# Gate and up products of two feed-forward networks with the weights as the stationary operand

## The chip, the cores and the metric

The kernel runs on one core of one Trainium2 chip. The metric is the device time of one execution in microseconds. Three runs of the kernel before gave a median of 2644.72 us (2642.13 to 2646.27). Traces come from one profiled execution, whose span, from the first to the last instruction, is 2638.1 us.

## What is computed

Two transformer blocks run one after the other on 256 tokens of width 2048, in float32. Each ends with a gated feed-forward network of hidden width 5632, and only these two networks are touched by the change:

```python
h2 = _rms(x, g_norm2) * (1 + sc2) + sh2                      # first block
gate, up = jnp.split(h2 @ w_ffn_in, 2, axis=-1)
x = x + gt2 * ((jax.nn.silu(gate) * up) @ w_ffn_out)
...
v = rmsnorm(h, ffn_norm_w)                                   # second block
h = h + (jax.nn.silu(v @ w_gate) * (v @ w_up)) @ w_down
return rmsnorm(h, final_norm_w)
```

## The kernel before

Names: P = 128, SEQ = 256 tokens, T = 2 token tiles of 128, CW = 512 columns, KD = 16 blocks of the width 2048, KF = 44 blocks of the hidden width.

**Split products.** Every float32 product is made of three fp32r products: operands are split into a high part, rounded to fp32r, and a low rest, and hi*hi, lo*hi and hi*lo are added in PSUM. A `Gemm` goes through chunks of 512 weight columns, and a chunk through slots of two 128-row blocks of the weights (k = 0, 1). A slot's raw weights (512 KB) are loaded by SyncE's queue into one of four buffers, ScalarE makes `w_hi` (`weights_high`, four buffers), VectorE makes `w_lo` (`weights_low`, two buffers). TensorE then issues 12 matmuls of a slot (lines 501 to 511): per k and token tile two with `w_hi` (token parts hi and lo), then per k and token tile one with `w_lo`. The tokens (`g.lhs`, 128 x 128) are the stationary operand and 512 weight columns stream past them. Output is 128 tokens by 512 columns, one PSUM bank for each token tile; chunks take turns between banks 0, 1 and banks 2, 3. With one chunk in flight, TensorE begins chunk c + 2 only when the banks of chunk c were read (line 487).

**Order.** Every engine runs its own hand-written instruction list; semaphores order them. What reads a finished chunk hangs as a hook in the list of ScalarE or VectorE, ahead of the weight conversion of slot `hook_at` = 4 of the following chunk. Chunks are written out one by one (`peeled` pairs) and then in a loop over pairs of chunks (`Fori`, line 103).

**The networks** (`Ffn`, line 1465). `self.g` has 22 chunks of 8 slots each, gate and up in turn: even chunks are gate, odd ones up. In the first network 5 pairs are written out and 6 go through the loop, in the second 2 and 9. The hook of a gate chunk (ScalarE, line 1572) writes silu(bank) to `ftmp`; that of an up chunk (VectorE, lines 1591 to 1597) writes `hbuf` = bank * `ftmp`, tokens on partitions. The product `self.down` (4 chunks of 22 slots) needs the hidden values with the hidden width on partitions, so `fill` (line 1551) makes TensorE turn the 8 blocks of a pair into `ps_turn`, in slot 2 of the next up chunk (`middle`, line 492), the last pair's in slot 4 of `down`. ScalarE's `high` and VectorE's `low` split what was turned into `ht_hi` and `ht_lo`. In the second network the tokens' inverse root mean square is left out of the product and is multiplied in when gate and up chunks are read, as a scalar per partition. ScalarE computes its squares beside slot 7 of the first chunk.

Of the kernel before, what the change touches and what calls it, by code (L numbers as in the profile page):

```python
# [11 lines left out]
ALU = mybir.AluOpType  # L12
# [33 lines left out]
class Gemm:  # L46


    def __init__(self, at, weights, k, n, lhs, cols=None, peeled=PEELED, k0=0):
# [11 lines left out]
        self.hook_at = min(4, 3 * self.S // 4)  # L61
# [83 lines left out]
def program(nc, A, out):  # L145
# [258 lines left out]
    def scalar_gemm(act, g, evac, carried=None, ahead=0):  # L404
# [7 lines left out]
        def chunk(u, j, before):  # L412
            for s, w in g.slots(u, j):
                if s == g.hook_at and before and g.S != 2:
# [41 lines left out]
    def tensor_gemm(pe, g, middle=None):  # L456
# [26 lines left out]
        def chunk(u, j, before):  # L483
# [4 lines left out]
            for s, w in g.slots(u, j):  # L488
# [3 lines left out]
                if s == g.S // 4 and before and middle:  # L492
                    middle(u - 1, j)
# [6 lines left out]
                pe.wait_ge(hi_ready, (w + 1).value)  # L500
                for k in range(2):
                    for t in range(T):
                        for part in range(2):
                            pe.matmul(bank[t][:, :], g.lhs(part, g.k0 + 2 * s + k, t), w_hi[:, w % HI, k, :],  # L504
                                      start=(s == 0 and k == 0 and part == 0), stop=False)
                pe.wait_ge(raw_used, (w + 1).value)
                for k in range(2):
                    for t in range(T):
                        mm = pe.matmul(bank[t][:, :], g.lhs(0, g.k0 + 2 * s + k, t), w_lo[:, w % LO, k, :],  # L509
                                       start=False, stop=(s == g.S - 1 and k == 1))  # L510
                mm.then_inc(w_used, 1)
# [3 lines left out]
        return lambda: middle(g.n - 1, None)  # L515
# [155 lines left out]
    def row_tensor(pe, n, bank):  # L671
        pe.wait_ge(diag_ready, 2 * n + 2)
        pe.matmul(bank[:, 0:SEQ], ones, diag[:, :, :].rearrange("p t q -> p (t q)"),
                  start=True, stop=True).then_inc(row_filled, 1)

    def diag_vector(dve, inv):
        for t in range(T):
            dve.tensor_scalar(diag[:, t, :], ident, inv(t), None, ALU.mult).then_inc(diag_ready, 1)

    def row_vector(dve, n, bank):  # L680
        dve.wait_ge(row_filled, n + 1)
        dve.tensor_copy(inv_row[:, :], bank[:, 0:SEQ]).then_inc(row_ready, 1)
# [721 lines left out]

    def evac_out(c, u, j):
# [19 lines left out]
    KF = 5632 // P  # L1425
    ht_hi = place("ht_hi", GT1, [KF, SEQ], F32R)
# [38 lines left out]
    class Ffn:  # L1465
# [4 lines left out]
        def __init__(self, name, w_gate, w_up, up0, w_down, scale, bias, gate, source=None, peeled=2):  # L1470
# [5 lines left out]
            self.g = Gemm(at, None, KD, 2 * KF // 4, lhs_x, cols=at_pair, peeled=peeled)  # L1476
            self.g.by_half = (w_gate, w_up)
            self.g.needs = self.turn.ready
            if source:
# [3 lines left out]
                turned_act, turned_dve = self.g.beside.act, self.g.beside.dve  # L1483
# [11 lines left out]
                self.g.beside.act, self.g.beside.dve = act_beside, dve_beside  # L1495
# [3 lines left out]
            self.at, self.at_split = turns["n"], turns["split"]  # L1499
            turns["n"] += KF // 2  # L1500
            turns["split"] += KF // 2
            self.down = Gemm(at, w_down, KF, 4, lhs_h, peeled=2)
            evac_down = evac_residual(self.down, gate)
# [8 lines left out]
            def down_needs(pe, s):  # L1512
                pe.wait_ge(turn_scaled, self.at + min(s + 1, KF // 2))

            def down_pe(pe, u, s):
                if (u, s) == (0, 4):
                    self.fill(pe, last_pair, Count(self.g.c + self.g.n))

            def down_act(act, u, s):
                if (u, s) == (0, 2) and gate is not None:  # L1520
                    gate_load(act, 1, gate)
                if (u, s) == (0, 7):
                    self.high(act, last_pair)

            def down_dve(dve, u, s):
                if (u, s) == (0, 7):
                    self.low(dve, last_pair)
            self.down.needs = down_needs
            self.down.beside.pe, self.down.beside.act, self.down.beside.dve = down_pe, down_act, down_dve

        def unit(self, pair, v):
            return (Count(self.at + 2 * pair.first + v, 2 * pair.per, pair.j),
                    Count(self.at_split + 2 * pair.first + v, 2 * pair.per, pair.j),
                    Count(4 * pair.first + 2 * v, 4 * pair.per, pair.j).value)

        def high(self, act, pair):
            for v in range(2):
                n, m, k = self.unit(pair, v)
                act.wait_ge(turn_filled, (n + 1).value)
                act.activation(ht_hi[:, bass.ds(k, 2), :].rearrange("p a b -> p (a b)"), ps_turn[v][:, :],  # L1540
                               ACT.Copy).then_inc(turn_hi, 1)

        def low(self, dve, pair):
            for v in range(2):
                n, m, k = self.unit(pair, v)
                dve.wait_ge(turn_hi, (m + 1).value)
                dve.tensor_tensor(ht_lo[:, bass.ds(k, 2), :].rearrange("p a b -> p (a b)"), ps_turn[v][:, :],
                                  ht_hi[:, bass.ds(k, 2), :].rearrange("p a b -> p (a b)").bitcast(F32),
                                  ALU.subtract).then_inc(turn_scaled, 1)

        def fill(self, pe, pair, c_end):
            pe.wait_ge(evac_done, c_end.value)
            for v in range(2):
                n, m, _ = self.unit(pair, v)
                pe.wait_ge(turn_scaled, (n - v).value)
                for k in range(2):
                    for t in range(T):
# [1389 lines left out]
```

## Time and profile before

| | |
|---|---|
| median of 3 runs | 2644.72 us |
| profiled execution, span | 2638.1 us |
| TensorE matmul busy | 98% of the span |
| TensorE weight load busy | 80% |
| VectorE busy | 63% |
| ScalarE busy | 45% |
| DMA | 212 GB/s mean over the span |
| granted TensorE clock, mean | 0.998 of 2.4 GHz |

Busy time of TensorE is modelled, since matmuls are pipelined: the distance from one start to the next is what tells its pace. "PEld" is TensorE's loading of a stationary operand, which runs beside the matmul before it. The chain of waits is the sequence of work that ended last, from the last instruction back to the first.

### The profile page before, as it was taken

How to read it: one execution, taken by the hardware profiler on the slowest of the kernel's cores; microseconds unless marked ns; L12 is line 12 of the kernel's file. 1: busy time of each engine (PE TensorE's matmuls, PEld its weight loads, DVE VectorE, ACT ScalarE, POOL GpSimd, SP SyncE). 2: the span in 40 equal slices, each digit the busy share in tenths (PEclk: the TensorE clock that was granted, in tenths of full speed). 3: DMA queues.
4: the chain of work that ended last, by engine and by line, in shares of the span. 5: the costliest groups of instructions: out<-in, count | busy, mean ns of one | idle time of the engine just before them, and what ended most of it. 6: DMA issues, size and time to landing. Idle time of an engine off the chain costs nothing.

```text
span 2638.1 us, 33116 instructions
## 1 busy us (share of the span) xinstructions
PE 2582.3 (98%) x12027; PEld 2118.6 (80%) x12027; DVE 1669.4 (63%) x2308; ACT 1194.3 (45%) x1595; POOL 149.2 (6%) x211
## 2 busy tenths in 40 slices
PE   5999999999999999999999999999999999999998
PEld 3888887878788888888888888776888888888887
DVE  7888998889877745454445664657645454454444
ACT  3543337644444444444334554446454444444443
POOL 1221111111111000000000000000000000000000
PEclk9999999999999999999999999999999999999999
DMA  9998994868788766666555655530666666665554
GB/s 347 318 304 268 312 320 155 283 203 314 250 265 279 244 185 191 189 189 203 194 194 185 188 171 178 172 116 17 183 184 191 191 186 191 189 190 188 195 192 168
DMA packets 269020, 559.41 MB, mean 212 GB/s; under 512 B 22800, under 2 KB 24544, under 8 KB 268256
## 3 DMA queue, kind: packets, MB, share of 16 engines
q1 hardware_dynamic: 235216, 454.23, 54.7%
q0 software_dynamic: 26752, 96.48, 11.0%
q10 hardware_dynamic: 6928, 7.07, 0.8%
q8 instruction: 75, 1.23, 0.2%
q14 instruction: 49, 0.40, 0.0%
HBM read 555.60 MB, written 2.11 MB: 211 GB/s over the span
## 4 chain that ended last, share of the span: by engine, by line
PE 94%; DVE 2%; ACT 1%; DMA 1%; issue 1%; SPq 0%; ACTq 0%; DVEq 0%
PE ps L504 57%; PE ps L509 28%; PE ps L545 1%; PE ps L1558 1%; DMA first_raw<-in_w_ada 1%; PE ps L2555 1%; PE ps L359 1%; PE ps L2402 1%; DMA ada_raw<-in_w_ada 1%; PE ps L2585 0%; PE ps L281 0%; SPq L319 0%; PE ps L2565 0%; PE ps L1269 0%; PE ps L2584 0%
## 5 line engine op out<-in xcount | busy, mean ns | idle before, releaser
L401 DVE TENSOR_TENSOR w_lo<-raw,w_hi 128x1024 fp32r<-128x1024 f32 x846 | 1033.7, 1223 | 824.5 <-PE ps L509 752.0
L395 ACT ACTIVATE w_hi<-raw 128x1024 fp32r<-128x1024 f32 x846 | 895.0, 1062 | 1146.8 <-PE ps L509 476.4
L504 PE MATMUL ps<-w_hi,xt_hi 128*128 128x512 f32 x2488 | 981.4, 394 | 4.8 <-ACT w_hi L395 1.6
L504 PE MATMUL ps<-w_hi,xt_lo 128*128 128x512 f32 x2488 | 969.8, 390 | 0.0
L509 PE MATMUL ps<-w_lo,xt_hi 128*128 128x512 f32 x2488 | 666.6, 390 | 3.9 <-DVE w_lo L401 3.9
L504 PEld LDWEIGHTS ps<-w_hi,xt_hi 128*128 128x128 f32 x2488 | 467.3, 188 | 105.6 <-issue 6.4
L509 PEld LDWEIGHTS ps<-w_lo,xt_hi 128*128 128x128 f32 x2488 | 466.5, 188 | 104.0 <-DVE w_lo L401 6.0
L504 PEld LDWEIGHTS ps<-w_hi,xt_lo 128*128 128x128 f32 x2488 | 467.6, 188 | 93.6
L504 PE MATMUL ps<-w_hi,ht_hi 128*128 128x512 f32 x696 | 271.6, 390 | 0.0
L504 PE MATMUL ps<-w_hi,ht_lo 128*128 128x512 f32 x696 | 270.9, 389 | 0.0
L509 PE MATMUL ps<-w_lo,ht_hi 128*128 128x512 f32 x696 | 186.1, 389 | 0.0
L319 POOL DMA_DIRECT2D ada_raw<-in_w_ada x192 | 138.8, 723 | 752.6 <-DVE acc_odd L343 588.7
L509 PEld LDWEIGHTS ps<-w_lo,ht_hi 128*128 128x128 f32 x696 | 130.7, 188 | 27.2
L504 PEld LDWEIGHTS ps<-w_hi,ht_hi 128*128 128x128 f32 x696 | 130.7, 188 | 26.9
L504 PEld LDWEIGHTS ps<-w_hi,ht_lo 128*128 128x128 f32 x696 | 130.7, 188 | 26.9
L343 DVE SCALAR_TENSOR_TENSOR acc<-ada_raw,ccol,acc 128x512 f32<-128x512 f32 (+1 forms) x171 | 119.9, 701 | 2.6 <-DMA ada_raw<-in_w_ada 2.5
L343 DVE SCALAR_TENSOR_TENSOR acc_odd<-ada_raw,ccol,acc_odd 128x512 f32<-128x512 f32 (+1 forms) x171 | 119.8, 701 | 0.0
L504 PE MATMUL ps<-w_hi,yt_hi 128*128 128x512 f32 x128 | 51.7, 404 | 0.0
L504 PE MATMUL ps<-w_hi,yt_lo 128*128 128x512 f32 x128 | 50.0, 391 | 0.0
L2799 POOL DMA_DIRECT2D w1k<-in_cmp_w_k x4 | 3.0, 752 | 732.9 <-PE ps L509 732.9
L1064 DVE TENSOR_TENSOR proj<-ps,proj 128x512 f32<-128x512 f32 x64 | 41.0, 681 | 3.1 <-PE ps L509 3.1
L2644 ACT ACTIVATE pb<-pb,nst 128x128 f32<-128x128 f32 x64 | 28.5, 447 | 29.6 <-DVE nst L2620 29.6
(398 smaller groups left out, 1590.1 us busy)
## 6 DMA issues: line engine op xcount, KB each, us to landing
raw<-in_w_in SPq DMA_DIRECT2D x208, 512.0 KB, 4.7
raw<-in_w_ffn_in SPq DMA_DIRECT2D x176, 512.0 KB, 4.1
ada_raw<-in_w_ada POOLq DMA_DIRECT2D x128, 512.0 KB, 5.6
raw<-in_w_ffn_out SPq DMA_DIRECT2D x88, 512.0 KB, 4.3
raw<-in_w_gate SPq DMA_DIRECT2D x88, 512.0 KB, 3.7
raw<-in_w_up SPq DMA_DIRECT2D x88, 512.0 KB, 4.4
raw<-in_w_down SPq DMA_DIRECT2D x88, 512.0 KB, 3.6
raw<-in_w_out SPq DMA_DIRECT2D x64, 512.0 KB, 4.7
```

Of the source, the lines that this page charges most:

```text
L319: sp.dma_start(self.tile(v), wview("w_ada")[:, ADA_K * s:ADA_K * (s + 1), col:col + width]).then_inc(ada_first[v] if v < 2 * self.per else ...
L343: ins = dve.scalar_tensor_tensor(part, rows[:, k, :], weight, part, ALU.mult, ALU.add)
L359: mm = pe.matmul(ps_ada[:, at_i:at_i + 1], acc[:, b % 2, i * P:(i + 1) * P], ones[:, 0:1], start=True, stop=True)
L395: act.activation(w_hi[:, w % HI, :, :], raw[:, w % RAW, :, :], ACT.Copy).then_inc(hi_ready, 1)
L401: dve.tensor_tensor(w_lo[:, w % LO, :, :], raw[:, w % RAW, :, :], w_hi[:, w % HI, :, :].bitcast(F32), ALU.subtract).then_inc(raw_used, 1)
L504: pe.matmul(bank[t][:, :], g.lhs(part, g.k0 + 2 * s + k, t), w_hi[:, w % HI, k, :], start=(s == 0 and k == 0 and part == 0), stop=False)
L509: mm = pe.matmul(bank[t][:, :], g.lhs(0, g.k0 + 2 * s + k, t), w_lo[:, w % LO, k, :], start=False, stop=(s == g.S - 1 and k == 1))
L545: mm = pe.transpose(ps_turn[n % 3][:, k * SEQ + t * P:k * SEQ + (t + 1) * P], self.src(2 * v + k, t), ident)
L1064: last = nc.vector.tensor_tensor(p, ps_gemm[2 * (c % 2) + t][:, :], p, ALU.add)
L1558: mm = pe.transpose(ps_turn[v][:, k * SEQ + t * P:k * SEQ + (t + 1) * P], hbuf[:, t, (2 * v + k) * P:(2 * v + k + 1) * P], ident)
L2402: mm = pe.matmul(ps_ada[0:60, 0:256], fl[i][:, u, :, :].rearrange("p h i -> p (h i)"), w1[i][:, u, :], start=(u == 0), stop=(u == 15))
L2644: act.activation(pb2[:, i % 4, lo:up], pb2[:, i % 4, lo:up], ACT.Exp, bias=nst[:, 1, 2 * i + t:2 * i + t + 1], scale=nsa_scale, accum_out= ...
```

## The change

In the gate and up products of both networks the operands change places. A 128 x 128 block of the weights is loaded as the stationary operand, and the 256 tokens of one 128-row block of the turned input stream past it. A slot is now 24 matmuls with 256 streamed columns each, in `turned`, in place of 12 with 512. A PSUM bank then holds two 128-column blocks of output, each 128 hidden columns by 256 tokens, so the output comes out turned. `fill`, `middle` and the turns are gone; `high` and `low` read `hbuf` in SBUF and are in other hooks: `high` of a pair in the next gate chunk's hook (first network) or in its own up chunk's (second network), `low` in the next gate chunk's. The last pair's are beside slots 4 and 5 of `down`, or in its carried hook.

In the second network tokens are now along the free axis, so their inverse root mean square is made into a row: two diagonal blocks on VectorE and one fp32 matmul by ones on TensorE in slot 0 of the second chunk, one copy on VectorE. VectorE multiplies gate chunks by that row into `ftmp`, ScalarE does silu in place, VectorE multiplies by the up chunk; the up side's factor is put off to the reading of `down` (`evac_scaled`, `final_add`). VectorE's hook is at slot 2 and ScalarE's at slot 6 there.

```diff
+        def turned(bank, s, w):
+            out = lambda m: bank[m // 2][:, m % 2 * SEQ:(m % 2 + 1) * SEQ]
+            pe.wait_ge(hi_ready, (w + 1).value)
+            for k in range(2):
+                for m in range(4):
+                    for part in range(2):
+                        pe.matmul(out(m), w_hi[:, w % HI, k, m * P:(m + 1) * P], g.turned(part, g.k0 + 2 * s + k),
+                                  start=(s == 0 and k == 0 and part == 0 and m % 2 == 0), stop=False)
+            pe.wait_ge(raw_used, (w + 1).value)
+            for k in range(2):
+                for m in range(4):
+                    mm = pe.matmul(out(m), w_lo[:, w % LO, k, m * P:(m + 1) * P], g.turned(0, g.k0 + 2 * s + k),
+                                   start=False, stop=(s == g.S - 1 and k == 1 and m % 2 == 1))
+            mm.then_inc(w_used, 1)
...
-                if s == g.S // 4 and before and middle:
-                    middle(u - 1, j)
...
+                (turned if g.turned else straight)(bank, s, w)
...
+    def evac_scaled(g, inv):
+
+        def evac(c, u, j):
+            for t in range(T):
+                xc = x[:, t, bass.ds(Count(CW * u, 2 * CW, j).value, CW)]
+                last = nc.vector.scalar_tensor_tensor(xc, ps_gemm[2 * (c % 2) + t][:, :], inv(t), xc, ALU.mult, ALU.add)
+            last.then_inc(evac_done, 1)
+        return evac
...
-            self.g = Gemm(at, None, KD, 2 * KF // 4, lhs_x, cols=at_pair, peeled=peeled)
+            self.g = Gemm(at, None, KD, 2 * KF // 4, None, cols=at_pair, peeled=peeled)
+            self.g.turned = lambda part, k: (xt_lo if part else xt_hi)[:, k, :]
...
+                self.g.hook_at, self.g.act_hook_at = 2, 6
...
+                def pe_beside(pe, u, s):
+                    turned_pe(pe, u, s)
+                    if (u, s) == (1, 0):
+                        row_tensor(pe, 2, ps_ada, diag2)
...
-                    if (u, s) == (1, 2):
-                        self.rms.vector(dve)
+                    if (u, s) == (1, 0):
+                        diag_vector(dve, self.rms.vector(dve), diag2)
...
             def down_needs(pe, s):
-                pe.wait_ge(turn_scaled, self.at + min(s + 1, KF // 2))
+                pe.wait_ge(self.h_lo, min(s + 1, KF // 2))
...
-        def fill(self, pe, pair, c_end):
-            pe.wait_ge(evac_done, c_end.value)
-            for v in range(2):
-                n, m, _ = self.unit(pair, v)
-                pe.wait_ge(turn_scaled, (n - v).value)
-                for k in range(2):
-                    for t in range(T):
-                        mm = pe.transpose(ps_turn[v][:, k * SEQ + t * P:k * SEQ + (t + 1) * P],
-                                          hbuf[:, t, (2 * v + k) * P:(2 * v + k + 1) * P], ident)
-                mm.then_inc(turn_filled, 1)
...
             def evac(c, u, j):
+                if u % 2:
+                    return
+                act.wait_ge(evac_done, c.value)
+                for v in range(2):
+                    last = act.activation(ftmp[:, v, :], ps_gemm[2 * (c % 2) + v][:, :], ACT.Silu)
+                last.then_inc(evac_done, 1)
+                if j is not None or u > 0:
+                    self.high(act, Count(u // 2 - 1, 1, j))
+
+            def evac_scaled_gate(c, u, j):
+                act.wait_ge(evac_done, (c + 1).value)
                 if u % 2 == 0:
...
+                    for v in range(2):
+                        last = act.activation(ftmp[:, v, :], ftmp[:, v, :], ACT.Silu)
+                    last.then_inc(self.silu_done, 1)
+                else:
+                    self.high(act, Count(u // 2, 1, j))
...
+                pair = Count(u // 2, 1, j)
                 if u % 2 == 0:
+                    if j is not None or u > 0:
+                        self.low(dve, pair - 1)
+                    if self.source:
+                        if j is None and u == 0:
+                            row_vector(dve, 2, ps_ada, inv_row2)
+                        else:
+                            dve.wait_ge(evac_done, c.value)
+                        for v in range(2):
+                            last = dve.tensor_tensor(
+                                ftmp[:, v, :].rearrange("p (m q) -> p m q", m=2),
+                                ps_gemm[2 * (c % 2) + v][:, :].rearrange("p (m q) -> p m q", m=2),
+                                inv_row2[:, None, :].broadcast_to([P, 2, SEQ]), ALU.mult)
+                        last.then_inc(evac_done, 1)
                     return
...
-            def middle(u, j):
-                if u % 2 == 0 and (j is not None or u > 0):
-                    self.fill(pe, Count(u // 2 - 1, 1, j), Count(self.g.c + u, 2, j))
-            tensor_gemm(pe, self.g, middle)()
+            tensor_gemm(pe, self.g)
             tensor_gemm(pe, self.down)
```

## Rows read from the trace of the kernel before

**Rows 1.** The page: busy times (1), the chain that ended last (4).

```profile
PE 2582.3 (98%) x12027; PEld 2118.6 (80%) x12027; DVE 1669.4 (63%) x2308; ACT 1194.3 (45%) x1595; POOL 149.2 (6%) x211
...
PE 94%; DVE 2%; ACT 1%; DMA 1%; issue 1%; SPq 0%; ACTq 0%; DVEq 0%
```

**Rows 2.** Chain of waits, first network's loop: start us, us, what.

```profile
1014.39 1.83 PE ps L504 x8
...
1018.94 0.91 PE ps L509 x4
1019.84 1.81 PE ps L504 x8
1021.66 0.91 PE ps L509 x4
...
1057.93 0.87 PE ps L1558 x8
1058.81 1.38 PE ps L504 x6
```

**Rows 3.** Line 1558 alone: durations ns min/median/max, first and last start.

```profile
L1558 PE MATMUL ps<-const,hbuf x176: 270/273/274, 788.2 to 2403.7; 128*128 128x128 f32 x176
```

**Rows 4.** Chain of waits around the narrow products of line 281.

```profile
405.22 2.73 PE ps L281 x24
407.95 0.87 PE ps L545 x8
408.82 2.76 PE ps L281 x24
```

**Rows 5.** Chain of waits, the second narrow product.

```profile
1544.10 5.46 PE ps L281 x48
```

**Rows 6.** Timeline, TensorE's matmuls and then its loads: start us, us, instruction.

```profile
1549.28 0.28 PE L281 MATMUL ps<-xt_lo,w_in_rest_hi 128*64 128x256 f32 x1
1549.39 0.40 PE L504 MATMUL ps<-w_hi,xt_hi 128*128 128x512 f32 x1
...
1549.28 0.19 PEld L504 LDWEIGHTS ps<-w_hi,xt_hi 128*128 128x128 f32 x1
```

**Rows 7.** Timeline, 930.2 to 931.2: a small load beneath a 512-column matmul.

```profile
930.01 0.84 PE L509 MATMUL ps<-w_lo,xt_hi 128*128 128x512 f32 x3
930.69 0.27 PE L959 MATMUL ps<-const,acol 128*16 128x128 f32 x1
```

**Rows 8.** Timeline, 830 to 831: loads of 128 columns, one streamed column each.

```profile
829.92 0.86 PEld L359 LDWEIGHTS ps<-const,acc 128*128 128x128 f32 x7
```

**Rows 9.** Timeline of ScalarE, VectorE and TensorE, start of the second network.

```profile
1921.77 0.30 ACT L716 ACTIVATE stat<-stat,epsc 128x2 f32<-128x2 f32 x1
...
1923.05 2.36 DVE L401 TENSOR_TENSOR w_lo<-raw,w_hi 128x1024 fp32r<-128x1024 f32 x2 [4.11 <-PE ps L509]
1926.27 1.23 DVE L401 TENSOR_TENSOR w_lo<-raw,w_hi 128x1024 fp32r<-128x1024 f32 x1 [0.86 <-PE ps L509]
1927.41 0.16 DVE L726 RECIPROCAL stat<-stat 128x2 f32<-128x2 f32 x1
...
1926.00 0.39 PE L504 MATMUL ps<-w_hi,xt_hi 128*128 128x512 f32 x1
```

**Rows 10.** Lines 673, 678 and 682, the same steps for another norm.

```profile
L673 PE MATMUL ps<-diag,const x4: 379/431/483, 33.2 to 710.3; 128*128 128x256 f32 x4
...
L678 DVE TENSOR_SCALAR diag<-const,stat x4: 280/284/288, 32.6 to 709.6; 128x128 f32<-128x128 f32 x4
...
L682 DVE COPY inv_row<-ps x2: 416/420/423, 35.1 to 710.7; 128x256 f32<-128x256 f32 x2
```

**Rows 11.** Groups by line, second network's loop: busy us, mean ns, idle before.

```profile
L395 ACT ACTIVATE w_hi<-raw 128x1024 fp32r<-128x1024 f32 x154 | 163.7, 1063 | 244.1 <-PE ps L509 154.4 <-DMA raw<-in_w_up 85.6 <-DMA raw<-in_w_gate 4.0
L1572 ACT ACTIVATE ftmp<-ps,stat 128x512 f32<-128x512 f32 x18 | 11.2, 675 | 0.0
L1540 ACT ACTIVATE ht_hi<-ps 128x512 f32 (+1 forms) x20 | 10.7, 584 | 0.0
...
L401 DVE TENSOR_TENSOR w_lo<-raw,w_hi 128x1024 fp32r<-128x1024 f32 x154 | 188.5, 1224 | 215.2 <-PE ps L509 213.7 <-ACT w_hi L395 1.5
L1594 DVE SCALAR_TENSOR_TENSOR hbuf<-ps,stat,ftmp 128x512 f32<-128x512 f32 x20 | 14.0, 743 | 0.0
L1547 DVE TENSOR_TENSOR ht_lo<-ps,ht_hi 128x512 f32 (+1 forms) x20 | 12.8, 679 | 0.0
```

**Rows 12.** DMA view: TensorE's instruction queue (packets, MB), two DMA issues (KB, us to landing).

```profile
q8 instruction: 75, 1.23, 0.2%
...
w2k<-in_cmp_w_k ACTq DMA_DIRECT2D x1, 64.0 KB, 7.4
const<-in_const SPq DMA_DIRECT2D x1, 128.0 KB, 2.2
```

**Rows 13.** Line 103, the loops' ends, on TensorE's sequencer.

```profile
L103 PEldq COMPARE_BRANCH  x15: 76/208/231, 982.4 to 2385.6; - x15
```

More of the change, by code:

```diff
@@ L413, in chunk @@
             for s, w in g.slots(u, j):
-                if s == g.hook_at and before and g.S != 2:
+                if s == g.act_hook_at and before and g.S != 2:
                     hook(u - 1, j)
@@ L454, in vector_gemm, with tensor_gemm, straight @@
         return lambda: hook(g.n - 1, None)
-    def tensor_gemm(pe, g, middle=None):
+    def tensor_gemm(pe, g):
+        def turned(bank, s, w):
[12 more added lines that the diff above has]
+            mm.then_inc(w_used, 1)
+        def straight(bank, s, w):
+            pe.wait_ge(hi_ready, (w + 1).value)
+            for k in range(2):
+                for t in range(T):
+                    for part in range(2):
+                        pe.matmul(bank[t][:, :], g.lhs(part, g.k0 + 2 * s + k, t), w_hi[:, w % HI, k, :],
+                                  start=(s == 0 and k == 0 and part == 0), stop=False)
+            pe.wait_ge(raw_used, (w + 1).value)
+            for k in range(2):
+                for t in range(T):
+                    mm = pe.matmul(bank[t][:, :], g.lhs(0, g.k0 + 2 * s + k, t), w_lo[:, w % LO, k, :],
+                                   start=False, stop=(s == g.S - 1 and k == 1))
+            mm.then_inc(w_used, 1)
         def by_tokens(c, u, w):
@@ L499, in chunk @@
                     g.needs(pe, s)
-                pe.wait_ge(hi_ready, (w + 1).value)
-                for k in range(2):
-                    for t in range(T):
[L503 to L511, printed above, removed]
+                (turned if g.turned else straight)(bank, s, w)
                 if j is None:
@@ L1403, in program @@
     evac_out1 = evac_residual(g_out, gt1)
+    def evac_scaled(g, inv):
+        def evac(c, u, j):
+            for t in range(T):
+                xc = x[:, t, bass.ds(Count(CW * u, 2 * CW, j).value, CW)]
+                last = nc.vector.scalar_tensor_tensor(xc, ps_gemm[2 * (c % 2) + t][:, :], inv(t), xc, ALU.mult, ALU.add)
+            last.then_inc(evac_done, 1)
+        return evac
     def evac_out(c, u, j):
@@ L1425, in program @@
     KF = 5632 // P
+    diag2 = place("diag2", SCR + 5120, [T, P])
+    inv_row2 = place("inv_row2", SCR + 4096, [SEQ])
     ht_hi = place("ht_hi", GT1, [KF, SEQ], F32R)
@@ L1521, in down_act @@
                     gate_load(act, 1, gate)
-                if (u, s) == (0, 7):
+                if (u, s) == (0, 4) and not source:
+                    act.wait_ge(evac_done, self.g.c + self.g.n)
                     self.high(act, last_pair)
             def down_dve(dve, u, s):
-                if (u, s) == (0, 7):
+                if (u, s) == (0, 5):
                     self.low(dve, last_pair)
             self.down.needs = down_needs
-            self.down.beside.pe, self.down.beside.act, self.down.beside.dve = down_pe, down_act, down_dve
+            self.down.beside.act, self.down.beside.dve = down_act, down_dve
         def unit(self, pair, v):
-            return (Count(self.at + 2 * pair.first + v, 2 * pair.per, pair.j),
-                    Count(self.at_split + 2 * pair.first + v, 2 * pair.per, pair.j),
+            return (Count(2 * pair.first + v + 1, 2 * pair.per, pair.j),
                     Count(4 * pair.first + 2 * v, 4 * pair.per, pair.j).value)
@@ L1584, in evac @@
             def evac(c, u, j):
+                pair = Count(u // 2, 1, j)
                 if u % 2 == 0:
[L1586 to L1597 removed]
+                    if j is not None or u > 0:
[11 more added lines that the diff above has]
+                        last.then_inc(evac_done, 1)
+                    return
+                if self.source:
+                    dve.wait_ge(self.silu_done, (pair + 1).value)
+                else:
+                    dve.wait_ge(evac_done, c.value)
+                for v in range(2):
+                    last = dve.tensor_tensor(hbuf[:, v, :], ps_gemm[2 * (c % 2) + v][:, :], ftmp[:, v, :], ALU.mult)
                 last.then_inc(evac_done, 1)
[L1599 to L1600 removed]
             last = vector_gemm(dve, self.g, evac, carried, 0)
```

74 lines of the change are left out of this document (22 added, 52 removed).

## Prediction

> **What bounds the kernel now.** I read the page's busy times first, then its chain of waits: TensorE's matmuls are busy 98% of the span and 94% of the chain is TensorE [rows 1]. So only what TensorE does, or what makes it wait, counts; VectorE at 63% and ScalarE at 45% are cover as long as they stay ahead. Then I read the chain in order of time inside the first network's loop, for the pace. A slot of gate or up takes 1.81 + 0.91 = 2.72 us for 12 matmuls with 512 streamed columns, 226.7 ns each [rows 2]. A pair of chunks, from one group of turns to the next, takes 1058.81 - 1014.39 = 44.42 us, and 16 slots are 43.52 us, so 8 turns with the transitions around them cost 0.90 us [rows 2]. The change has three questions: what goes with the turns, what the new shape of matmul costs, and whether anything new is late.
>
> **Turns removed.** 176 turns are 22 groups of 8 [rows 3]. They stand in TensorE's own list with nothing beside them: 22 x 0.90 = 19.8 us off the path.
>
> **24 matmuls of 256 columns for 12 of 512.** There are 2 x 22 x 8 = 352 slots and the streamed columns stay at 6144, but the loads of a stationary 128 x 128 block double. No row has 256 fp32r columns over a 128-column load in a run, so I bound the pace from both sides.
> - Stream: line 281 streams 256 fp32r columns over 64-column loads, 5.46 us for 48, or 113.75 ns each, as in the first 24 of another [rows 4, 5]; 24 right behind turns took 2.76 us, 115.0 ns each [rows 4]. Half of 226.7 is 113.3, so the cost is nearly all per column. Over all 96 the mean is 10.95 / 96 = 114.06 ns.
> - Load: with one streamed column above them, seven loads of 128 columns take 0.86 us, a last one 0.19 us, so they follow each other at (0.86 - 0.19) / 6 = 112 ns [rows 6, 8]. This is just below the stream's 113.3.
> - Do they nest? At the end of line 281 a 128-column load of line 504 starts with a 256-column matmul at 1549.28, and the next matmul starts at 1549.39, 0.11 us later [rows 6]. In the opposite case the third of three 512-column matmuls has a load of only 16 columns beneath it, and the three still take 0.68 us, 227 ns each [rows 7]. So a lighter load doesn't quicken the stream and a heavier one, once, didn't slow it.
>
> The pace is the larger of 113.3 and 112, with a little for jitter in so tight a fit. I take 113.5 ns, between a half of 226.7 and the 113.75 that holds a few slower starts: 24 x 113.5 - 2720 = 4 ns a slot, 352 slots, +1.3 us. Ends: 113.3 gives 0, and 116.5 gives (2796 - 2720) x 352 = +26.8 us.
> The Trainium skill, "TensorE: Matmul & The Clock Gate", section "Back-to-back issue gap", speaks against the change: a warm matmul takes its columns at 2.4 GHz and a fixed 2.5 ns. By that a slot would gain 12 x 2.5 = 30 ns, an estimate of +10.6 us. The trace shows 227 and 114 ns, where the page would have 216 and 109; as 512a + f and 256a + f they give f = 2 x 114.06 - 226.7 = 1.4 ns.
>
> **The row in the second network.** TensorE gets one fp32 matmul by ones; the same form took 379 to 483 ns [rows 10]: +0.45 us. It also gets a wait for VectorE's diagonals, and all its later matmuls are queued behind that. The root is done at 1922.07 and slot 0 of the second chunk ends at 1926.00 [rows 9]. VectorE makes the first `w_lo` from 1923.05 to 1924.27, then 0.16 for the reciprocal and 2 x 0.28 for the diagonals: 1925.0, 1.0 us ahead of need [rows 9, 10]. The next `w_lo` slips by 0.7 us and is still done at 1926.2, while its matmuls start 1.81 us into the slot. The copy of the row takes 0.42 us on VectorE and waits for TensorE's matmul at about 1926.9; it and two multiplications end near 1928.8, and the `w_lo` behind them at 1930.0, needed at 1931.0. All hidden, bounds 0 to +1 us.
>
> **VectorE's and ScalarE's hooks.** They cost 0, and the cover is this. VectorE can start a `w_lo` when the slot two before it ends, 2.72 + 1.81 us ahead of need; less its 1.22 us that leaves 3.3 us. The heaviest new hook (second network, gate) is two `low` at 0.68 and two multiplications by a row, a form not in the trace, between 0.68 and 0.74 each: 2.84 us [rows 11]. It starts 1.22 us into the chunk and ends at 4.06, where the next `w_lo` could have begun at 2.72: 1.34 of the 3.3 us are used. In the first network a hook has two instructions on VectorE, before it had four. ScalarE is up to four slots ahead, and its heaviest hook, four activations of about 0.58 us, takes 2.3 of more than 9 us; silu from SBUF is not shown, but silu and copies from PSUM took 0.58 to 0.68 [rows 11]. A gate result now passes VectorE, ScalarE, VectorE, with 8 slots for it. SyncE's loads wait for `w_lo` as before; ScalarE's idle time before `w_hi` ends partly on DMA [rows 11], with slots in hand. Reading `down` costs 0.74 in place of 0.68 us, hidden save for the last one at the end: +0.05 us. If this cover were gone, each hook's overrun would count 22 times.
>
> **Sum.** -19.8 + 1.3 + 0.45 + 0.05 = -18.0 us against the profiled span of 2638.1, or 2620.1. Around the span lie 2644.72 - 2638.1 = 6.6 us to the median of the runs, which stay: 2627 us.
>
> **Rivals.**
> - *Each matmul has a fixed part after all.* f from 1.4 to 6 ns, times 4224 additional matmuls, is +5.9 to +25 us in place of 1.3: 2632 to 2651. For it: 115.0 ns behind turns is f = 3.3 [rows 4], and only 1 ns lies between load and stream. Against it: 48 in a row at 113.75 [rows 5]. From f = 4.6 ns nothing is left of the gain. At the page's 2.5 ns it is 2636. Chance 0.20.
> - *The load slows the stream: slower than before.* 226.7 is 13.4 ns above 512 columns at 2.4 GHz, and 113.75 about 7 above 256. The matmul of 512 has a load of 128 columns and that of 256 one of 64, so the surplus could come from the load. Then 256 over 128 is 106.7 + 13.4 = 120 ns, +160 ns a slot, +56 us: 2682. It decides from 115.6 ns on. Against it stand the two single cases of [rows 6, 7]. Chance 0.08.
> - *The loop no longer stays in instruction memory: slower too.* A loop turn grows from 16 x 24 + 16 = 400 loads and matmuls to 768. Of 24,054 executed [rows 1], 13 repeats of 400 leave 18,850, and the queue brought 1.23 MB [rows 12], which is 65 bytes for each of these: repeats were not fetched again, and the branch takes 208 ns [rows 13]. How much more is held no row shows. A miss at each of 13 branches costs one transfer, 2.2 to 7.4 us [rows 12]: +29 to +96 us, 2656 to 2723. The skill's page "Runtime: NRT & Kernel Launch", section "Instruction fetch mechanics", has a taken branch stall when its target is out of a two-page window, with pages of 256 instructions, but gives TensorE room for 2048. By the window the old loop of 400 was near the limit and the new one is beyond it; by the room it fits. Chance 0.07.
> - *A new wait*, on the diagonals or behind the 2.84 us hook: once up to 3 us, or 22 times up to 1 us, 2628 to 2649. Chance 0.05.
> - *The turns go but other transitions of TensorE stay*, some 3 us less gain: 0.02.
>
> **Numbers.** The forecast, 2625 to 2632 (pace 113.3 to 114.06), has 0.58. Under 2622 there is almost nothing, since 19.8 us is all that is removed. The range goes up to 2654, over the fixed part and the new wait; the two slow cases, 0.15, stay out. About 0.2%, 5.3 us, is what a measurement can tell from no change. Faster: 0.58 + 0.08 of the fixed part + 0.03 of the new wait + 0.02 = 0.71. Same: 0.09 + 0.02 = 0.11. Slower: 0.03 + 0.08 + 0.07 = 0.18.
>
> **What would show it.** No turn of `hbuf`; 8448 matmuls of 128x256 in gate and up with starts 113 to 114 ns apart, a slot still 2.72 us and a pair 43.5; no idle time of TensorE ended by VectorE at the start of the second network; TensorE's instruction queue silent inside the loops. A slot of 2.77 us would be the fixed part, 2.88 the load, a gap of some us once a loop turn the instructions.

## The result, and the profile after

The kernel after takes 2681.26 us (median of 4 runs, 2678.53 to 2681.91), that before, beside it, 2645.32 us: a ratio of 1.0136, with a 95% interval of 1.0121 to 1.015. The change costs 36 us, where 18 us of gain were forecast. The profiled execution has a span of 2679.2 us. It is 41.1 us over that of before, but 5 of these lie ahead of the changed code: the row matmul of the norm before the first network starts at 715.2 us, that of before at 710.3 [rows 10]. The program up to there is the same; from 25 to 75 us TensorE's granted clock was 0.86 of full speed in this execution, part of it at 1.2 GHz, and 1.00 in that of before.

The page of after, busy times, the chain that ended last and TensorE's instruction queue, as [rows 1, 12]:

```profile
PE 2625.6 (98%) x16077; PEld 2328.4 (87%) x16077; DVE 1685.5 (63%) x2333; ACT 1192.8 (45%) x1595; POOL 149.5 (6%) x211
...
q8 instruction: 88, 1.44, 0.2%
...
PE 96%; DVE 1%; ACT 1%; DMA 1%; issue 1%; SPq 0%; ACTq 0%; DVEq 0%
```

The chain of waits in the first network's loop, as [rows 2] (line 465 is the products with `w_hi`, line 470 those with `w_lo`):

```profile
1016.11 1.92 PE ps L465 x16
1018.03 0.96 PE ps L470 x8
1018.99 1.92 PE ps L465 x16
1020.91 0.96 PE ps L470 x8
```

There are no turns between chunks any more, and no gap. But a slot takes 1.92 + 0.96 = 2.88 us for 24 matmuls, 120.0 ns each, in place of 2.72. It does so from the first chunk of the first network to the last of the second: 352 x 0.16 = 56.3 us more, less 19.8 us for the turns, is 36.5 us, the whole loss. The costliest groups of loads and matmuls (busy us, mean ns of one, idle time before):

```profile
L465 PE MATMUL ps<-xt_hi,w_hi 128*128 128x256 f32 x2816 | 692.3, 284 | 1.0 <-issue 1.0
...
L465 PEld LDWEIGHTS ps<-xt_hi,w_hi 128*128 128x128 f32 x2816 | 540.4, 192 | 1.5 <-issue 1.4
...
L479 PEld LDWEIGHTS ps<-w_hi,xt_hi 128*128 128x128 f32 x1080 | 204.1, 189 | 51.3 <-ACT w_hi L396 5.6
```

In the products that kept their form (line 479) TensorE's loading side has idle time before its instructions; in the turned ones (line 465) it has next to none, 1.5 us over 2816 loads. That alone doesn't tell what sets the pace: the run load_64 below, at 113.3 ns a matmul, has next to none either. No matmul of gate and up waits for VectorE or ScalarE. The new steps at the start of the second network, VectorE's timeline, answer to [rows 9]: the copy of the row waits 0.90 us for TensorE, the two multiplications take 0.64 each, and the `w_lo` behind them makes nobody wait.

```profile
1950.50 0.42 DVE L698 COPY inv_row<-ps 128x256 f32<-128x256 f32 x1 [0.90 <-PE ps L689]
1950.96 1.29 DVE L1618 TENSOR_TENSOR ftmp<-ps,inv_row 128x512 f32<-128x512 f32 x2
1952.16 2.43 DVE L402 TENSOR_TENSOR w_lo<-raw,w_hi 128x1024 fp32r<-128x1024 f32 x2
```

### The profile page after: what moved, and what is told of

It reads as the page before. It is cut to its first block, busy times and chain, and to the rows that moved or that the text cites. A ratio compares the mean times of both kernels' runs of the same rounds, so it can differ in the third digit from the quotient of the medians.

```text
span 2679.2 us, 41186 instructions
## 1 busy us (share of the span) xinstructions
PE 2625.6 (98%) x16077; PEld 2328.4 (87%) x16077; DVE 1685.5 (63%) x2333; ACT 1192.8 (45%) x1595; POOL 149.5 (6%) x211
## 3 DMA queue, kind: packets, MB, share of 16 engines
q8 instruction: 88, 1.44, 0.2%
## 4 chain that ended last, share of the span: by engine, by line
PE 96%; DVE 1%; ACT 1%; DMA 1%; issue 1%; SPq 0%; ACTq 0%; DVEq 0%
PE ps L479 33%; PE ps L465 25%; PE ps L484 16%; PE ps L470 13%; PE ps L561 1%; DMA first_raw<-in_w_ada 1%; PE ps L2581 1%; PE ps L360 1%; PE ps L2428 1%; PE ps L2611 0%; SPq L320 0%; PE ps L282 0%; PE ps L2591 0%; PE ps L2610 0%; PE ps L2026 0%
## 5 line engine op out<-in xcount | busy, mean ns | idle before, releaser
L465 PE MATMUL ps<-xt_hi,w_hi 128*128 128x256 f32 x2816 | 692.3, 284 | 1.0 <-issue 1.0
L465 PE MATMUL ps<-xt_lo,w_hi 128*128 128x256 f32 x2816 | 690.8, 283 | 0.0
L465 PEld LDWEIGHTS ps<-xt_hi,w_hi 128*128 128x128 f32 x2816 | 540.4, 192 | 1.5 <-issue 1.4
L465 PEld LDWEIGHTS ps<-xt_lo,w_hi 128*128 128x128 f32 x2816 | 540.5, 192 | 0.1
L479 PE MATMUL ps<-w_hi,xt_hi 128*128 128x512 f32 x1080 | 431.7, 400 | 5.8 <-ACT w_hi L396 4.7
L479 PE MATMUL ps<-w_hi,xt_lo 128*128 128x512 f32 x1080 | 423.2, 392 | 0.0
L470 PE MATMUL ps<-xt_hi,w_lo 128*128 128x256 f32 x2816 | 395.3, 283 | 0.0
L470 PEld LDWEIGHTS ps<-xt_hi,w_lo 128*128 128x128 f32 x2816 | 363.3, 192 | 0.0
L484 PE MATMUL ps<-w_lo,xt_hi 128*128 128x512 f32 x1080 | 289.8, 390 | 0.8 <-DVE w_lo L402 0.8
L484 PEld LDWEIGHTS ps<-w_lo,xt_hi 128*128 128x128 f32 x1080 | 203.0, 188 | 44.5 <-DVE w_lo L402 1.4
```

Source lines behind the costliest of these rows:

```text
L465: pe.matmul(out(m), w_hi[:, w % HI, k, m * P:(m + 1) * P], g.turned(part, g.k0 + 2 * s + k), start=(s == 0 and k == 0 and part == 0 and m ...
L470: mm = pe.matmul(out(m), w_lo[:, w % LO, k, m * P:(m + 1) * P], g.turned(0, g.k0 + 2 * s + k), start=False, stop=(s == g.S - 1 and k == 1 ...
```

## The experiments

The theory was now the rival of 0.08: the surplus over pure streaming (13.3 ns for each matmul) is paid by every matmul above a 128-column load, however few columns it streams. Against it stood other causes for the same 2.88 us: twice the instructions, the turned form's addresses or banks, the removal of the turns itself.

**pace: TensorE alone.** Series of matmuls of one shape each, with nothing beside them.

```diff
+            for i in range(2 * N):        # N = 240; series of other sizes alike
+                pe.matmul(ps[i % 4][:, 0:256], wr[:, at(i, 128):at(i, 128) + 128], xr[:, 0:256], start=True, stop=True)
+            for i in range(2 * N):
+                pe.matmul(ps[i % 4][0:64, 0:256], wr[:, at(i, 128):at(i, 128) + 64], xr[:, 0:256], start=True, stop=True)
```

> Nothing of the kernel is computed here: TensorE alone runs series of 240 or 480 independent matmuls, each with its own stationary load, and the distance of starts in each is read. Theory A, the surplus belongs to the loaded columns: a matmul of N streamed fp32r columns with S stationary ones takes N / 2.4 + S / 9.6 ns. Theory B, a load of 128 columns needs 120 ns and the stream 1.0625 x N / 2.4, and the larger counts. Theory C, TensorE's instruction stream gives one instruction in 60 ns, so a load and a matmul take at least 120 ns. N=512: S=128 all 226.7; S=64 A 220, B and C 226.7; S=32 A 216.7, B and C 226.7. N=384, S=128: A 173.3, B and C 170. N=256: S=128 all 120; S=96 A 116.7, B 113.3, C 120; S=64 A and B 113.3, C 120; S=32 A 110, B 113.3, C 120. N=128, S=128: A 66.7 or the load's 112, B 120, C 120. bf16 with 128 stationary columns, 512 and 256 streamed: 215.5 and 109 by rows of the kernel before where only the first is shown; C 120 for the second. Alternating 128 and 64 stationary columns at N=256 tells which matmul of the two carries the surplus.

It took 658.54 us. Its chain of waits, one piece a series (start us, us, matmuls):

```profile
39.88 31.28 PE ps L50 x138
```

```profile
71.61 55.20 PE ps L52 x240
126.81 55.60 PE ps L54 x240
182.41 41.62 PE ps L56 x240
224.03 57.59 PE ps L58 x480
281.62 27.84 PE ps L60 x240
309.46 54.41 PE ps L62 x480
363.87 27.20 PE ps L64 x240
391.07 28.79 PE ps L66 x240
419.86 26.22 PE ps L68 x240
```

```profile
623.08 26.75 PE ps L87 x240
```

Each line divided by its count gives the distance of two starts. fp32r, 512 streamed columns: 226.7 ns over a load of 128 (line 50), 230.0 over 64 (line 52), 231.7 over 32 (line 54). 384 over 128: 173.4 (line 56). 256 columns: 120.0 over 128 (line 58), 116.0 over 96 (line 60), 113.35 over 64 (line 62), 113.3 over 32 (line 64); with the same block loaded each time 120.0 (line 66). bf16, 256 over 128: 109.25 (line 68). fp32r, 128 over 128: 111.5 (line 87). So 120.0 and 113.35 ns both come back with TensorE alone: the loss has nothing to do with this kernel's queues, banks or DMA. The row of line 281 that the forecast went by is right, for its loads of 64 columns.

None of the three theories holds throughout. C is out, since 116.0 and 113.35 ns lie under its 120. B is out by 384 columns (173.4 against 170) and by 96 loaded ones (116.0 against 113.3). A is within 1 ns for loads of 64 to 128 columns beneath 256, and for 384 over 128. But at 32 loaded columns it gives 110 where 113.3 was measured, and at 512 streamed ones it has narrower loads quicken the stream, 220 and 216.7, where they slow it, 230.0 and 231.7. The alternating series (lines 73 and 75, 256 columns) should have told whether a surplus goes with a matmul's own width or with the load beneath it. By the start times the next matmul comes 116.4 ns behind a 128-wide one with a 64-column load beneath it, and 117.0 ns behind a 64-wide one with a 128-column load beneath it. Both are near the mean of 120.0 and 113.35, so the series doesn't tell. In every series the load and the matmul that uses it are equally wide, so "width of the load" below always means both.

**no_turns: the change without its form.** The turns stay out, but gate and up products keep the old form, tokens loaded and 512 weight columns streamed.

```diff
-            self.g = Gemm(at, None, KD, 2 * KF // 4, None, cols=at_pair, peeled=peeled)
-            self.g.turned = lambda part, k: (xt_lo if part else xt_hi)[:, k, :]
+            self.g = Gemm(at, None, KD, 2 * KF // 4, lhs_x, cols=at_pair, peeled=peeled)
```

> The changed kernel with the old form of matmul in gate and up (tokens stationary, 512 streamed columns); its output is not the reference's, since what is read as turned is not turned. It has the turns removed, the row and the new hooks. If the step on the turns was right, it takes 2645.3 - 19.8 + 0.5 = 2626 us, and the whole loss of the change, 2681.3 - 2626 = 55 us, is the form of the matmuls. If hooks or the new wait cost something, it is above 2626 by that much.

2624.67 us (2622.4 to 2626.39), ratio 0.9929 (0.9908 to 0.9949). Its chain in the loop:

```profile
1001.20 1.81 PE ps L479 x8
1003.01 0.91 PE ps L484 x4
1003.92 1.81 PE ps L479 x8
```

The slot is 2.72 us again and the gain of the turns is there: 17 us under the 2641.84 of before beside it, 13 to 24 by the interval. The new hooks, the row and the wait are in this kernel too, and cost nothing that shows: 2626 was expected with 0.5 us for them. The loss, 57 us from here to after, is the matmul's form.

**load_96: 96 of 128 weight columns.** The turned products load 96 columns and so make 96 of 128 hidden columns; all else stays.

```diff
-                        pe.matmul(out(m), w_hi[:, w % HI, k, m * P:(m + 1) * P], g.turned(part, g.k0 + 2 * s + k),
+                        pe.matmul(out(m)[0:96], w_hi[:, w % HI, k, m * P:m * P + 96], g.turned(part, g.k0 + 2 * s + k),
```

> The changed kernel with only 96 of each 128 weight columns loaded in gate and up, so a quarter of the hidden values is not computed; number of matmuls, streamed columns, waits and DMA stay. Theory A (surplus per loaded column): 116.7 ns, 24 x 3.33 x 352 = 28 us less than 2681: 2653. Theory B (load-bound): 113.3 ns, 56 us less: 2625. Theory C (instruction stream): 120 ns, 2681.

2647.93 us (2641.41 to 2655.8), ratio 1.0021 (1.0008 to 1.0033).

```profile
1001.43 1.85 PE ps L465 x16
1003.28 0.93 PE ps L470 x8
```

2.78 to 2.79 us a slot, 116 ns a matmul, the 116.0 of line 60. Same instructions, addresses and streamed columns as after, with fewer loaded columns: the time falls by 33 us. It is nearest to theory A, by which the surplus grows with the loaded columns (2653), 5 us below it.

**half_the_loads: hi and lo tokens over one load.** They lie next to each other, and one load of a `w_hi` block is followed by one matmul with 512 streamed columns: 8 matmuls of 512 and 8 of 256 in a slot. The first block (k = 0) of each chunk's first slot keeps its pairs of 256, 4 of the 8 pairs of one slot in eight.

```diff
-                    for part in range(2):
-                        pe.matmul(out(m), w_hi[:, w % HI, k, m * P:(m + 1) * P], g.turned(part, g.k0 + 2 * s + k),
-                                  start=(s == 0 and k == 0 and part == 0 and m % 2 == 0), stop=False)
+                    if s == 0 and k == 0:
+                        for part in range(2):
+                            pe.matmul(out(m), w_hi[:, w % HI, k, m * P:(m + 1) * P], g.turned(part, g.k0 + 2 * s + k),
+                                      start=(part == 0 and m % 2 == 0), stop=False)
+                        continue
+                    pe.matmul(bank[m // 2][:, :], w_hi[:, w % HI, k, m * P:(m + 1) * P],
+                              xt_both[:, :, g.k0 + 2 * s + k, :], start=False, stop=False)
```

> The changed kernel with the high and the low part of the tokens streamed as one matmul of 512 columns over one load of w_hi, into a whole bank; the two halves are not added, so the output is not the reference's. A slot has 8 matmuls of 512 and 8 of 256 columns: 16 loads in place of 24. Theory A: 8 x 226.7 + 8 x 120 = 2773 ns in place of 2880, 38 us less than 2681: 2644. Theory B: a load beneath 512 columns is free, one beneath 256 takes 120, also 2773 ns and 2644. Theory C: 8 x 226.7 + 8 x 120 as well, or 2720 ns and 2625 if the queue evens the pairs out. It tells what the change would cost with its loads shared.

2650.11 us (2647.77 to 2652.32), ratio 1.0024 (1.0014 to 1.0034).

```profile
1000.25 1.84 PE ps L469 x8
1002.09 0.95 PE ps L474 x8
1003.04 1.84 PE ps L469 x8
```

Nearly a third fewer matmuls over 128 columns take 31 us off, where 37 were expected. The pairs that stay are 44 x 4 x 13.3 ns = 2 us of the difference. The price per matmul holds for most of the rest. The matmuls of 512 took 230 ns here and not 226.7, which is 8 x 3.3 ns x 352 = 9 us; those of 256, at 119 and not 120, give 3 of them back. In the kernel before the eight matmuls of 512 behind the turns are slower in the same way, 1.83 us where later slots have 1.81 [rows 2], and the first five behind line 281's [rows 6] start 229 to 236 ns apart. So a change of shape or type seems to slow the matmuls of 512 behind it, and here one comes in every slot. No run varies that alone.

**pace2: what the surplus belongs to.** TensorE alone again: other lengths, plain fp32, 64 partitions, accumulation in one bank with moving addresses, and bf16 and fp32r by turns, in which load and matmul above it are of different types.

```diff
+            for i in range(N):
+                if i % 2:
+                    pe.matmul(ps[i % 4][:, 0:256], wr[:, at(i, 128):at(i, 128) + 128], xr[:, 0:256], start=True, stop=True)
+                else:
+                    pe.matmul(ps[i % 4][:, 0:256], wb[:, at(i, 128):at(i, 128) + 128], xb[:, 0:256], start=True, stop=True)
```

> Nothing of the kernel is computed; series of 240 matmuls of TensorE alone, as in the run pace. That run showed a surplus over N / 2.4 of 13.3 ns for fp32r with 128 loaded columns at N = 256, 384 and 512, a distance of 112 ns at N = 128, and only 2.5 ns for bf16. Theory D, shared reading: an fp32r stream takes TensorE's whole reading rate, so what a load of 128 fp32r columns reads beneath it comes on top, 13.3 ns, and a stream that leaves room (bf16, fp32 in its passes) hides it. Theory A, own load: the surplus belongs to the fp32r matmul itself, whatever is loaded beneath. Taking turns of bf16 and fp32r, N=256: D 112 for the bf16 matmul (the fp32r load beneath it limits) and 107 to 110 for the fp32r matmul (light bf16 load beneath it), about 220 for two; A 109 + 120 = 229 or, limited by the load, 232. The same at N=512: D 215.5 + 215 to 220, A 215.5 + 226.7 = 442. fp32r, 128 loaded columns: N=192 the load's 112 (80 + 13.3 = 93 is hidden), N=224 112 (93.3 + 13.3 = 106.7), N=320 146.7 by both. fp32 N=256: 215 to 219 a pass, as line 2555 in the kernel before. 112 loaded columns at N=256: 118.3 if in proportion. 64 partitions in place of 128: 120 by both. One bank with accumulation and moving source addresses: 120 by both, other than 120 if the surplus is a matter of addresses or banks. One bf16 in three at N=256: D 112 + 120 + 109, A 109 + 2 x 120 = 349.

```profile
101.64 26.78 PE ps L60 x240
128.42 26.82 PE ps L62 x240
155.24 35.20 PE ps L64 x240
190.44 51.80 PE ps L66 x240
242.24 28.27 PE ps L68 x240
270.50 28.98 PE ps L70 x240
299.49 28.98 PE ps L72 x240
```

192 columns over 128 take 111.6 ns (line 60), 224 take 111.75 (line 62), 320 take 146.7 (line 64). 256 over 112 loaded take 117.8 (line 68). The plain fp32 series issues 120 matmuls of 256 columns and its trace has 240, so each runs as two of 215.8 ns, 431.7 together (line 66). Neither 64 partitions (line 70) nor one bank and moving addresses (line 72) change the 120 ns: 120.75 both, with the start of the series in it. The mixed series missed every expected value. 120 pairs of lines 51 and 53 lie between 15.3 and 46.1 us, 0.26 us a pair; in the first 5 us the starts lie nearly twice as far apart, and after them a pair takes 244 ns, where 120.0 + 109.25 = 229 would be nothing new. With 512 columns a pair takes 460 ns (theory D 430 to 436, A 442), and one bf16 and two fp32r of 256 take 360 (D 341, A 349). Changing the type costs some 11 to 18 ns there and back, as much as what was to be told apart or more, so it stays open whether the surplus belongs to the fp32r matmul or to the fp32r load beneath.

**load_64: 64 of 128 weight columns,** with the shape of the row that the forecast went by. The edit is that of load_96 with 64.

```diff
+                        pe.matmul(out(m)[0:64], w_hi[:, w % HI, k, m * P:m * P + 64], g.turned(part, g.k0 + 2 * s + k),
```

> The changed kernel with only 64 of each 128 weight columns loaded in gate and up, so half of the hidden values is not computed; all else stays. In the run pace 256 fp32r columns over 64 loaded columns took 113.3 ns, as line 281 does in the kernel before, and 120.0 over 128. If the step that failed is that line 281's pace belongs to its 64-column loads, this kernel has the pace of the prediction: a slot of 2720 ns and 2681 - 352 x 0.16 = 2625 us. If the 120 ns came from the number of instructions or from what DMA, VectorE and ScalarE do beside, it stays at 2681.

2624.15 us (2622.18 to 2649.78), ratio 0.9952 (0.991 to 0.9995). Three of the four executions lie within 3 us; the fourth took 25 us more at the same granted clock, 0.995, and nothing recorded says why.

```profile
1002.31 1.81 PE ps L465 x16
1004.13 0.91 PE ps L470 x8
```

```profile
L465 PEld LDWEIGHTS ps<-xt_hi,w_hi 128*64 128x64 f32 x2816 | 377.4, 134 | 1.9 <-issue 1.8
```

2.72 us a slot for 24 matmuls: this is the time that was forecast (span 2621.7, against a sum of 2620.1), with the same count of instructions and the same DMAs as after. Only the width of the load, and with it of the matmul's output, differs. So the failed step is the one that took a pace over 64 loaded columns for one over 128.

**pace3: bf16 for a part, in groups.** If changes of type are rare, bf16's smaller surplus could be had for the two low products.

```diff
+            for g in range(30):
+                for i in range(8):
+                    pe.matmul(ps[i % 4][:, 0:256], wr[:, at(i, 128):at(i, 128) + 128], xr[:, 0:256], start=True, stop=True)
+                for i in range(16):
+                    pe.matmul(ps[i % 4][:, 0:256], wb[:, at(i, 128):at(i, 128) + 128], xb[:, 0:256], start=True, stop=True)
```

> Nothing of the kernel is computed; TensorE alone, 30 groups each of 4 fp32r and 8 bf16 matmuls of 512 columns, 8 fp32r and 16 bf16 of 256, 8 fp32r and 4 bf16 of 512, all over 128 loaded columns. The run pace had 226.7 and 120.0 ns for fp32r, 215.5 and 109.2 for bf16; the run pace2 had 460 ns for one of each with 512 and 244 with 256 columns, so a change of type costs some 17 ns there and back. If that cost comes once a group: 4 x 226.7 + 8 x 215.5 + 17 = 2648 ns; 8 x 120 + 16 x 109.2 + 15 = 2722 ns; 8 x 226.7 + 4 x 215.5 + 17 = 2693 ns; the all-fp32r slots take 2720 and 2880. If it comes otherwise, the groups differ by that.

```profile
61.11 0.93 PE ps L51 x4
62.04 1.74 PE ps L53 x8
```

```profile
140.13 1.76 PE ps L58 x16
141.90 0.95 PE ps L56 x8
```

```profile
225.35 0.88 PE ps L63 x4
226.23 1.85 PE ps L61 x8
```

4 fp32r and 8 bf16 of 512 take 2.67 us (2.648 expected), 8 fp32r and 16 bf16 of 256 take 2.71 (2.722), 8 fp32r and 4 bf16 of 512 take 2.73 (2.693). Right for 256 columns, 1% too low for 512: behind a change of type the fp32r matmuls of 512 took 231 to 233 ns in place of 226.7. The first group is what the old form of gate and up would issue with its low products in bf16.

**low_in_bf16: a version that beats both.** The turned form stays. The high product stays in fp32r (8 matmuls a slot), the two low ones (16) take bf16 copies of the high parts and low parts in bf16. ScalarE makes the copies.

```diff
+                    pe.matmul(out(m), w_hi[:, w % HI, k, m * P:(m + 1) * P], xt_hi[:, kk + k, :],
+                              start=(s == 0 and k == 0 and m % 2 == 0), stop=False)
+            for k in range(2):
+                for m in range(4):
+                    pe.matmul(out(m), w_hi16[:, w % HI, k, m * P:(m + 1) * P], xt_16[:, kk // 2, 1, k, :],
+                              start=False, stop=False)
...
-                    mm = pe.matmul(out(m), w_lo[:, w % LO, k, m * P:(m + 1) * P], g.turned(0, g.k0 + 2 * s + k),
+                    mm = pe.matmul(out(m), w_lo16[:, w % LO, k, m * P:(m + 1) * P], xt_16[:, kk // 2, 0, k, :],
```

> The kernel after with its turned form kept, but of the three products of a split gate or up block only the high one (8 matmuls of 256 columns) stays in fp32r; the two low ones (16 matmuls) take bf16 copies of the high parts and bf16 low parts. Nothing is left out. ScalarE makes the bf16 copy of each block's high part (one more instruction of 128x1024 per slot) and of the turned tokens; the gate loads and the final block's modulation are read one slot later. If the loss is the surplus of fp32r matmuls over 128 loaded columns: TensorE alone did such a group of 24 in 2.713 us where the kernel after needs 2.880, so 352 x 0.167 = 59 us less than 2681: 2622, and up to 2630 with the start of each network, where ScalarE has to make the copies of the tokens first. If ScalarE can't keep up (its two conversions of about 1.06 us each and the hooks beside them, in slots of 2.72 us): a wait of the high products for w_hi shows in the slots that carry hooks, and the time stays above 2640. If the surplus were in the turned form and not in the number format: 2681.

2623.82 us (2620.44 to 2630.21), before beside it 2644.4, ratio 0.9935 (0.9913 to 0.9956): 21 us under before and 57 under after. The chain in the loop, and the groups of the loads:

```profile
1002.82 0.95 PE ps L471 x8
1003.77 0.89 PE ps L475 x8
1004.66 0.87 PE ps L480 x8
```

```profile
L471 PE MATMUL ps<-xt_hi,w_hi 128*128 128x256 f32 x2816 | 420.3, 292 | 5.7 <-ACT w_hi L401 4.5
...
L480 PEld LDWEIGHTS ps<-xt,w_lo 128*128 128x128 bf16 x2816 | 275.5, 98 | 31.9
```

The slot is 2.72 us (1005.54 - 1002.82), as pace3 gave it. A bf16 load takes 98 ns where one of fp32r takes 192, and the loading side has idle time again. ScalarE keeps up but for the first chunk of a network, where it also copies the tokens; in all TensorE waits 4.5 us for it in line 471. ScalarE's timeline in the first chunk:

```profile
720.13 1.04 ACT L400 ACTIVATE w_hi<-raw 128x1024 bf16<-128x1024 f32 x1
721.07 1.04 ACT L401 ACTIVATE w_hi<-raw 128x1024 fp32r<-128x1024 f32 x1
722.02 0.89 ACT L631 ACTIVATE xt_hi<-tmp,acol 128x256 fp32r<-128x256 f32 x2
722.94 0.63 ACT L600 ACTIVATE xt<-xt_hi 128x512 bf16<-128x512 f32 x1
723.48 1.04 ACT L400 ACTIVATE w_hi<-raw 128x1024 bf16<-128x1024 f32 x1
```

That is 3.35 us a slot (723.48 - 720.13), above TensorE's 2.72. The low products now carry bf16's precision, which a user has to weigh. As no_turns takes 2624.67 us with the old form, the gain of both over before is that of the turns, and bf16 only pays for the form that makes the turns needless. A rival wasn't run: bf16 for the low products in the old form, with its turns. By pace3's 2.67 us for 4 fp32r and 8 bf16 matmuls of 512 it would save 352 x 0.05 = 18 us, an estimate of 2627, nearly as much without the change.

## Why the prediction was wrong, step by step

**Turns, -19.8 us: right.** no_turns shows 17 us (13 to 24), and 22 x 0.90 is in it.

**24 matmuls of 256 for 12 of 512, +1.3 us: wrong, +56.3 us.** The step that failed is the pace of a 256-column matmul over a 128-column load, put at 113.5 ns from a row with 64-column loads; it is 120.0. This one term is the whole miss (4 ns x 352 is also 1.4 us and not 1.3, which changes nothing): with it the sum is -19.8 + 56.3 + 0.45 + 0.05 = +37.0 us; measured are 2681.26 - 2645.32 = 36 us. Three readings went into it.
- The stream's bound was read from line 281 [rows 4, 5], 113.75 ns over loads of 64 columns, and set beside 226.7 ns over loads of 128 [rows 2]. Two things differ between these rows. "Half of 226.7 is 113.3, so the cost is nearly all per column" and f = 1.4 ns came out of that mixture. With one load width, 120.0 and 226.7 give f = 2 x 120.0 - 226.7 = 13.3 ns (pace, lines 58 and 50). load_64 has the width of line 281 and gave the forecast's time.
- "A heavier one, once, didn't slow it" [rows 6] read one distance, 0.11 us, from a view with steps of 0.01 us, where 0.113 or 0.120 was asked. The finer start times do have 113 ns there, so the event was real; but one 64-wide matmul over a single wide load isn't a stream of 128-wide ones, which takes 120.0.
- "A lighter load doesn't quicken the stream" [rows 7] was true at 512 columns, and more so than it seemed: there loads of 64 and 32 make it slower (230.0 and 231.7 ns). But it was carried over to 256 columns, where 120.0 falls to 113.35.

The load's bound, 112 ns [rows 8], was right: 111.5 to 111.75 ns for 128, 192 and 224 streamed columns. What failed was to take the larger of two bounds as the pace. The ends of the range for this term, 113.3 to 116.5, were drawn around the row of another shape, so the range missed 120.0, though the rival had worked it out.

The Trainium skill, "TensorE: Matmul & The Clock Gate", section "Step-by-step: what each phase is for", says that loading the next weights takes no reading bandwidth from the running matmul. The pace of a 256-column fp32r matmul here depends on the load's width, 113.35 ns over 64 and 120.0 over 128, so whoever takes every load for free by that sentence is 6.7 ns short. Whether it is the load beneath or the wider matmul itself that costs them, and whether reading has to do with it, no run shows. By the section "Back-to-back issue gap" of the Trainium skill's same page, weighed in the forecast, a matmul has 2.5 ns beside its columns; the section gives this for an isolated matmul. bf16 has that here (109.25 - 106.7 = 2.6 ns); fp32r over 128 has 13.3.

**The row, the hooks, the wait, +0.5 us: right.** No matmul of gate and up waits for VectorE. TensorE's part of the row took 0.43 us against 0.45, in part by luck: the forecast took the duration of one recorded matmul (379 to 483 ns) for the row, and the row is two records 216 ns apart. The copy and the multiplications took 0.42 and 2 x 0.64 us, forecast as 0.42 and 2 x 0.68 to 0.74.

**The rivals.** *The load slows the stream*, 0.08, gave slot 2.88 us and 2682 us; measured 2.88 and 2681.26. The argument for it was the stronger one, since it explained both rows' surplus with one rule (13.4 over 128, 7 over 64), and it was set aside for two single events. Its number was right; its mechanism isn't shown, since by its rule 512 columns over 64 would take 220 ns and they take 230.0. *A fixed part*: it is one, but of 13.3 ns and not 1.4 to 6. *Instruction memory*: didn't happen; the queue brought 1.44 MB against 1.23, for 8100 loads and matmuls more, none of it between 996 and 1246 us or between 2047 and 2429, which is behind each loop's first turn, and nothing waits at the loops' ends. By the window of two pages in the Trainium skill, "Runtime: NRT & Kernel Launch", section "Instruction fetch mechanics", which the forecast weighed, a loop of 768 should have stalled; the trace agrees with the larger room that the section gives TensorE. *A new wait* and *transitions stay*: neither.

## What to carry to other kernels

Before a pace is taken over from another row, compare all of its sizes, the loaded columns too: with fp32r, 256 columns over a 128-column load cost 6% more per column than 512, so prefer the form with the longest stream for each load, if nothing else differs. If a rival explains all regular rows and only single events speak against it, the regular rows should have the higher chance. Removing a side cost (here 0.90 us per pair of chunks) doesn't pay for 7 ns on each of thousands of matmuls: 384 matmuls a pair x 6.7 ns is 2.6 us.

## What the runs showed of the hardware that was not expected

- fp32r over a load of 128 columns: about 111.6 ns at 128, 192 and 224 streamed columns N, and N / 2.4 + 13.3 ns at those from 256 to 512 (120.0 at 256, 146.7 at 320, 173.4 at 384, 226.7 at 512).
- At 256 streamed columns the surplus over 106.7 ns follows the width of the load: 13.3 ns at 128, 11.1 at 112, 9.3 at 96, 6.7 at 64, where it ends (6.6 at 32). At 512 it goes the other way: 13.4 at 128, 16.7 at 64, 18.4 at 32. No theory here explains both, and that stays open, as does whether the load or the matmul of that width pays.
- bf16 has 2.6 ns at 256 columns. A plain fp32 matmul of 256 columns runs as two recorded ones of 215.8 ns, 431.7 together, where three fp32r products take 3 x 120.0 = 360.
- Going from bf16 to fp32r and back costs about 15 ns a pair at 256 columns, and the fp32r matmuls of 512 behind it are slower by 4 to 6 ns each. The same slowing follows a change of shape in one type (230 ns in half_the_loads, 229 to 236 ns behind line 281's matmuls in the kernel before).
